# Window attention in two layers: score products from four-byte operands to rounded part and residual

## The reference, cut to what matters

```python
q, k, v, c, g = jnp.split(u @ w_in[i], splits, axis=-1)
q = rms_norm_2(q.reshape(B, S, N_HEADS, HEAD_DIM), q_norm[i])
k = rms_norm_2(k.reshape(B, S, KV_HEADS, HEAD_DIM), k_norm[i])
...
s = jnp.einsum('bnqkgd,bnskd->bnkgqs', qb, kw).astype(jnp.float32) * scale
...
s = s + bias[None, None]
s = jnp.where(valid[None, :, None, None], s, NEG_INF)
...
pr = jax.nn.softmax(jnp.concatenate([s, sink_l], axis=-1), axis=-1)[..., :-1]
o = jnp.einsum('bnkgqs,bnskd->bnqkgd', pr.astype(v.dtype), vw)
...
c = c_val * jax.nn.sigmoid(c_gate)
c = depthwise_conv(c, conv_w[i], conv_b[i])
```

## Time and profile before

| | |
|---|---|
| median of 3 runs | 2380.95 us (2372.4 to 2381.05) |
| profiled execution | 2381.47 us, span 2379.7 us |
| TensorE busy | 2258.0 us, 95% of the span |
| VectorE busy | 1733.5 us, 73% |
| ScalarE busy | 1232.8 us, 52% |
| mean granted TensorE clock | 0.986 |

### The profile page before, as it was taken

One profiled execution on the slowest core, in us unless ns is written; L12 is line 12 of the kernel. 1 busy time (PEld: TensorE's weight loads), 2 busy tenths in 40 slices (PEclk: granted clock), 3 DMA queues, 4 the chain that ended last, 5 costly groups with the idle time before them and its releaser, 6 DMA issues.

```text
span 2379.7 us, 38110 instructions
## 1 busy us (share of the span) xinstructions
PE 2258.0 (95%) x15380; PEld 2072.6 (87%) x15380; DVE 1733.5 (73%) x1813; ACT 1232.8 (52%) x1301; POOL 219.3 (9%) x199
## 2 busy tenths in 40 slices
PE   4999889999999998999999999999999999999999
PEld 4997788799889877799788997988998899798899
DVE  5997786796589976755677569977567756996665
ACT  2443555454454545455466454666456636466644
POOL 0123000010201300000021000011001100001200
PEclk9999999999999999899999999999999999999999
DMA  8996432586568752455455542445454554345453
GB/s 345 350 357 230 153 142 108 214 312 259 194 236 355 299 209 91 160 212 179 175 190 189 186 154 104 158 179 188 183 182 159 189 182 160 107 153 179 181 188 135
DMA packets 75934, 471.49 MB, mean 198 GB/s; under 512 B 8707, under 2 KB 8963, under 8 KB 27580
## 3 DMA queue, kind: packets, MB, share of 16 engines
q1 hardware_dynamic: 53136, 383.80, 43.7%
q0 software_dynamic: 18976, 68.71, 7.7%
q10 hardware_dynamic: 3724, 17.56, 2.0%
HBM read 468.97 MB, written 1.06 MB: 198 GB/s over the span
## 4 chain that ended last, share of the span: by engine, by line
PE 77%; DVE 12%; ACT 6%; DMA 3%; issue 2%; ACTq 0%; SPq 0%; DVEq 0%
PE ab L1848 30%; PE acc L1848 13%; PE acc L1987 9%; PE ab L1879 7%; PE mb L1879 6%; DVE wlo L1039 3%; PE ab L1881 3%; PE mb L1881 3%; ACT whi L471 2%; DMA raw<-stream 2%; PE mb L2234 1%; DMA par<-params 1%; DVE sc L1659 1%; PE acc L2262 1%; DVE sc L1130 1%
## 5 line engine op out<-in xcount | busy, mean ns | idle before, releaser
L1039 DVE TENSOR_TENSOR wlo<-raw,whi 128x2048 fp32r<-128x2048 f32 x361 | 827.3, 2295 | 317.2 <-ACT whi L471 315.2
L471 ACT ACTIVATE whi<-raw 128x2048 fp32r<-128x2048 f32 x361 | 689.4, 1912 | 472.9 <-DMA raw<-stream 297.7
L1848 PE MATMUL ab<-uu,whi 128*128 128x256 f32 x4512 | 830.4, 287 | 25.2 <-DVE uu L1227 11.7
L1848 PEld LDWEIGHTS ab<-uu,whi 128*128 128x128 f32 x4512 | 711.6, 194 | 40.1 <-issue 22.8
L1848 PE MATMUL ab<-uu,wlo 128*128 128x256 f32 x2256 | 643.2, 285 | 0.0
L1848 PEld LDWEIGHTS ab<-uu,wlo 128*128 128x128 f32 x2256 | 437.7, 194 | 0.0
L1848 PE MATMUL acc<-h_hi,whi 128*128 128x256 f32 (+1 forms) x1032 | 293.8, 285 | 4.3 <-ACT sc L853 1.6
L1848 PE MATMUL acc<-h_hi,wlo 128*128 128x256 f32 (+1 forms) x1032 | 292.4, 283 | 0.0
L1848 PE MATMUL acc<-h_lo,whi 128*128 128x256 f32 (+1 forms) x1032 | 292.4, 283 | 0.0
L1879 PE MATMUL ab<-uu,whi 128*128 128x512 f32 x704 | 252.0, 400 | 8.7 <-DVE uu L1323 4.9
L1879 PE MATMUL mb<-uu,whi 128*128 128x512 f32 x704 | 249.9, 398 | 0.0
(11 more groups left out here) (338 smaller groups left out, 2734.7 us busy)
## 6 DMA issues: line engine op xcount, KB each, us to landing
raw<-stream SPq DMA_DIRECT2D x365, 1024.0 KB, 4.8
modmem<-mods POOLq DMA_DIRECT2D x128, 512.0 KB, 6.1
sc<-lnrows ACTq DMA_DIRECT2D x5, 1024.0 KB, 5.2
sc<-start ACTq DMA_DIRECT2D x4, 1024.0 KB, 16.7
gateb<-gaterows ACTq DMA_DIRECT2D x6, 512.0 KB, 3.7
hank<-toep POOLq DMA_DIRECT2D x8, 192.0 KB, 3.8
x<-xT ACTq DMA_DIRECT2D x1, 1024.0 KB, 31.5
x<-xn ACTq DMA_DIRECT2D x1, 1024.0 KB, 4.8
```

The source lines that it names most:

```text
L471: nc.scalar.activation(whi[:, n % RAW, :], raw[:, n % RAW, :], ACT.Copy).then_inc(hi_ready, 1)
L1039: nc.vector.tensor_tensor(wlo[:, n % RAW, :], raw[:, n % RAW, :], whi[:, n % RAW, :].bitcast(F32), ALU.subtract).then_inc(lo_ready, 1)
L1848: ins = nc.tensor.matmul(out, l, r, start=first and i == 0, stop=last and i == 2, skip_group_check=True)
```

## The change

In `window(l)` each query and key tile gets a rounded copy in `h_hi` and a residual in `h_lo` (tiles 16 to 21 of both). ScalarE makes the copies, VectorE the residuals, in two portions: tiles 16 and 20 (heads 0 and 1 with their keys) first, the other four afterwards. Semaphores `cn_ready` and `cnhi_ready` carry the two hand-overs of each portion. TensorE waits for the first portion at `j == 1` and for the second at `j == 3`. In `qk` three products of split operands stand where one of four-byte operands stood.

```diff
+                        act.wait_ge(cn_ready, 2 + 2 * l + 1)
+                        for i in (0, 4):
+                            ins = nc.scalar.activation(h_hi[:, 16 + i, :], sc[:, 16 + i, :], ACT.Copy)
+                        ins.then_inc(cnhi_ready, 1)
+                        act.wait_ge(cn_ready, 2 + 2 * l + 2)
+                        for i, m in ((1, 3), (5, 1)):
+                            ins = nc.scalar.activation(h_hi[:, 16 + i:16 + i + m, :], sc[:, 16 + i:16 + i + m, :], ACT.Copy)
+                        ins.then_inc(cnhi_ready, 1)
...
-                        for i in range(6):
-                            gc = small[:, 0:1] if i < 4 else col("k_norm_2", l)
-                            ins = nc.vector.scalar_tensor_tensor(out=sc[:, 16 + i, :], in0=sc[:, 16 + i, :], scalar=gc,
-                                                                 in1=sc[:, 32 + i, :], op0=ALU.mult, op1=ALU.mult)
-                        ins.then_inc(wqk_ready, 1)
+                        def scale_qk(tiles):
+                            for i in tiles:
+                                gc = small[:, 0:1] if i < 4 else col("k_norm_2", l)
+                                ins = nc.vector.scalar_tensor_tensor(out=sc[:, 16 + i, :], in0=sc[:, 16 + i, :], scalar=gc,
+                                                                     in1=sc[:, 32 + i, :], op0=ALU.mult, op1=ALU.mult)
+                            return ins
+
+                        def rest_qk(parts):
+                            for i, m in parts:
+                                ins = nc.vector.tensor_tensor(h_lo[:, 16 + i:16 + i + m, :], sc[:, 16 + i:16 + i + m, :],
+                                                              h_hi[:, 16 + i:16 + i + m, :].bitcast(F32), ALU.subtract)
+                            return ins
+
+                        scale_qk((0, 4)).then_inc(cn_ready, 1)
+                        scale_qk((1, 2))
+                        dve.wait_ge(cnhi_ready, 2 + 2 * l + 1)
+                        rest_qk(((0, 1), (4, 1))).then_inc(wqk_ready, 1)
+                        scale_qk((3, 5)).then_inc(cn_ready, 1)
+                        dve.wait_ge(cnhi_ready, 2 + 2 * l + 2)
+                        rest_qk(((1, 3), (5, 1))).then_inc(wqk_ready, 1)
...
-                    return [(sc[r, 16 + h // 2, qb * P:qb * P + P], sc[r, 20 + h // 4, :], 0, T),
+                    qs, ks = slice(qb * P, qb * P + P), 20 + h // 4
+                    return [(h_hi[r, 16 + h // 2, qs], h_hi[r, ks, :], 0, T),
+                            (h_lo[r, 16 + h // 2, qs], h_hi[r, ks, :], 0, T),
+                            (h_hi[r, 16 + h // 2, qs], h_lo[r, ks, :], 0, T),
...
-                        pe.wait_ge(wqk_ready, 3 + l)
+                        pe.wait_ge(wqk_ready, 2 + 2 * l + 1)
                         pe.wait_ge(hanklo_ready, 1)
+                    if j == 3:
+                        pe.wait_ge(wqk_ready, 2 + 2 * l + 2)
```

## The result

| | before | changed |
|---|---|---|
| median of 11 runs | 2377.79 us (2372.4 to 2381.78) | 2384.35 us (2379.36 to 2394.83) |
| ratio | | 1.0032, 95% interval 1.0021 to 1.0043 |
| profiled execution | 2381.47 us, span 2379.7 | 2379.36 us, span 2377.5 |

The change costs 0.32%, 7.6 us (5.0 to 10.2 by the interval), less than the 0.5% that the prediction set as its bound. The forecast was 5.3 us. The profiled execution of the changed kernel is the fastest of its eleven and the one of the kernel before lies high among its own, so their times can't be set against each other. The attention stages can: their code is all that differs. I measure a stage from the start of VectorE's gain factor (L1686, after L1694) to the start of its subtraction of the convolution's mean (L1709, after L1735).

What follows compares the result with a forecast made beforehand. VectorE, 9.63 us a block against TensorE's 9.50, sets the stage's pace. Per layer 3.35 - 0.69 = 2.66 us, +5.3 for two: 2386.8 from the profiled 2381.47, stated as 2386; range 2383 to 2391, overall 2378 to 2396.

Steps and rivals of the forecast that it cites:

- its two waits: VectorE's only idle times for TensorE in the first attention stage, 2.23 and 0.69 us, capping what TensorE's saving could shorten.
- VectorE is late by 3.35 us: At the stage's head, scaling then subtracting in two portions delays VectorE: 2.1 us of work, 1.2 waiting for ScalarE's copies.
- its bounds: Limits on VectorE's delay: 2.1 us if the wait vanished, 3.8 if each of four hand-overs costs 0.1 more.
- The first score: TensorE may start head 0 at 1417.57 us, after the first portion's subtractions; it started at 1417.61 before.
- The wait at the fifth block: VectorE's wait for TensorE's weight block, 2.23 us in the first stage and 0.91 in the second, was to stay.
- the last one: VectorE's 0.69 us wait for TensorE near the loop's end was to go, leaving 2.66 us a layer.
- Three rounded products cost 0.36 us: TensorE's scores per head and query block, 0.63 us before: saving 0.27 each, 8.6 us over all (bounds -1 and 8.6).
- ScalarE's delay: ScalarE's weight rounding, behind the new copies, ends at 1421.4 us; VectorE wants it at 1421.43, so no other term.
- The chain of waits: It should bear VectorE's name to the loop's end, with no VectorE wait for TensorE after the fifth block.
- The clock: Rival, chance 0.19: TensorE idles earlier, low clock holds a whole weight block, costing 4.6 and 6.0 us; up to 2397.4.
- The new idle time of 3 us: TensorE waits for ScalarE's normalization of head 0 before its transposes, 3.3 us of idleness that were none.
- the second half of this rival: Before the next transposes TensorE waits about as long again as the 3.3 us before head 0's.

Runs made afterwards that it cites:

- Split only: The changed kernel keeping the split on VectorE and ScalarE, but taking scores from the four-byte tiles as before: ratio 1.0034 to the kernel before.
- products only: The kernel before with three rounded products in the scores and no split made, so scores are not those of queries and keys: ratio 1.0007 to the kernel before.
- grouped scores: The changed kernel with each head's six query-key products first, then four bias products, starting the bank anew once a head: ratio 1.0044 to the kernel before.
- the subtractions on GpSimd: The changed kernel with the split's four subtractions issued on GpSimd, VectorE only scaling: ratio 1.0035 to the kernel before.
- the wait filled: The changed kernel with VectorE scaling all six tiles in one go and block 1 before subtracting the second portion: ratio 1.0024 to the kernel before.

## Why the prediction was right, point by point

*VectorE is the limit, and TensorE's saving is worth only its two waits.* Right. Split only has the whole cost, products only and grouped scores have no gain, and less its waits for TensorE the stage is 95.1 us before and 98.4 after.

*VectorE is late by 3.35 us, 1.2 of it a wait.* Measured 3.27 and 1.22. The points on the way, counted from the first scaling, came within 0.1 us of the forecast. The range did not follow from its bounds: 2.1 and 3.8 us of delay give 2384.3 to 2387.7 us by the prediction's own sum, and it says 2383 to 2391.

*The first scores come at the same time.* Right: 2.48 us after the first scaling, 2.51 before.

*The wait at the fifth block stays, the last one goes.* Half right. The last is 0.20, not 0: the last transposes cost 0.66 us behind an idle moment and not 0.44. The other was 0 to 2.4 us in all kernels, the same code included. It is no constant, and the forecast's agreement with 5.1 us from the profiles contains this luck: layer 0 gained 1.1 by it, layer 1 lost 0.7. The kernel's 7.6 us has an interval of 5.0 to 10.2 that holds both numbers; whether there is more than the stages show stays open.

*Three rounded products cost 0.36 us.* Wrong, 0.54; the saving is 0.075 us a query block by the head's 2.12 and 1.97 (0.27 forecast), 2.4 us over all and not 8.6. The step that failed is the choice of the row: I took 0.12 us from products among their like and set aside the 0.22 around the bias products, as a matter of the four-byte neighbour. It is a matter of the change between 64 and 128 rows, which both kernels have. An estimate: without the steps around it (0.20 us of the 0.54) the old product took about 0.43 us, 3.6 rounded ones. So I was wrong against the Trainium skill too (FP8 and Floating Point Precision, TensorE Precision Notes, four passes for true FP32): a saving of 0.16 by its count was nearer than mine, and the row of 0.63 did not speak for more than four passes. It cost nothing only because the sum did not rest on it.

*ScalarE's delay is just covered.* Right for the changed kernel (the weight residual started 0.05 us behind its rounding, with no wait), and the words "the cover is just used up" were the important ones: two experiments in which VectorE came earlier ran straight into this wait (2.42 us with the subtractions on GpSimd, 0.51 with the wait filled).

*The chain of waits.* Wrong. It was to bear VectorE's name to the end of the loop, and it bears TensorE's from 1438 to 1502. The error is in how the chain was expected to name two full engines and not in who sets the pace.

*The clock.* The new idle time of 3 us ahead of the first transposes did not come (0 and 0.31 us), since the clock fell earlier than thought, at the first scores. Windows of the changed kernel:

```profile
1412.00:1414.00 2.00, 0.46 (x4) 0.26 (x3) 2.00 (x7) 0.72 (x2) 0.00 (x0) 1.00 0.50 66
1414.00:1416.00 2.00, 1.89 (x8) 1.44 (x8) 0.85 (x3) 1.12 (x3) 0.00 (x0) 0.72 0.74 311
1416.00:1421.00 5.00, 5.00 (x24) 4.86 (x24) 4.90 (x6) 4.95 (x5) 0.00 (x0) 0.50 0.14 59
```

TensorE was idle for 1.65 us ahead of them, as in the kernel before (1.68), where the clock stayed. The low level lasted until about 1421.7, so the greater part of block 2 ran at it, though not the whole, and filled the gap. VectorE had no wait at blocks 2 and 3. But the second half of this rival, a longer wait ahead of the next transposes, did come. The transposes of the changed kernel in layer 1:

```profile
2022.48 0.66 PE L2269 MATMUL acc<-par,sc 128*128 128x128 f32 x4 [0.31 <-ACT sc L772]
2035.02 1.12 PE L2269 MATMUL acc<-par,sc 128*128 128x128 f32 x4 [4.17 <-ACT sc L772]
```

The gap is 3.24 us in layer 0 and 4.17 in layer 1, 2.42 in both layers of the kernel before. In layer 1 VectorE's wait at the fifth block grew with it, from 0.91 to 1.60 us. That is 0.7 us and not the 6.0 that the rival had as its most, and in layer 0 the wait shrank. So the slowdown by the clock came true only in a small part, and that part lies within the spread of the same code.

## What to carry to other kernels

Where two engines are full over the same window, the chain of waits names one of them and is no help; count an engine's own time over several blocks and see which one drifts behind. An exchange of work between such engines is to be priced on the one that drifts, and then on the queue of every engine that the hand-over passes, since the next cover may be used up as well. If the work must be added there, move something else out of the stage into idle time just ahead of it: that brought this kernel level with the kernel before. Before reading a difference of two stages, take out the waits that vary between executions of the same code, and look at the granted clock in both.

## What the runs showed of the hardware that I had not expected

- A change of the number of rows between rounded products costs TensorE about 0.25 us each time: 1.97 us with four changes and 1.48 with two, for the same ten products. The grouped kernel also starts the bank anew once a head and not twice; that this costs nothing was not tried by itself.
- GpSimd at work slows VectorE's products with two operands in SBUF and a column of factors: 2.45 us for six becomes 4.05 to 4.97. The weight residual, a subtraction of two SBUF operands without such a column, mostly keeps its 2.28 us beside it (2.59 once), but another plain product of two SBUF operands took 1.23 us beside GpSimd's subtraction and 0.69 without. Where the weight residual keeps its time GpSimd's own instruction beside it is the longer one, 2.6 to 2.8 us where its neighbours take 0.7 to 0.8.
- The same idle gap of 1.65 to 1.7 us on TensorE is followed by the low clock in one execution and not in another of the same code (it falls in the second stage of the repetition of the kernel before, and not in the first stage of its first profile), and the low level then lasts from some 3 to some 7 us. Stages of the same code differ by up to 2.4 us, nearly all of it in the one wait at the fifth block.
